# Second mixture of a two-block network: per-group picks and gates, sums added straight into the residual, 20 weight slots in place of 16, and the output's first half spread and written before the second

## The reference, cut to what matters

```python
x = x + (gates[:, :, 0] * y_rwkv + gates[:, :, 1] * y_attn) @ w_out      # the merge
h2 = rmsnorm(x, norm2_g)
...
grp = argmax(h2 @ w_router_group + b)                 # one of 4 groups
exp_logits = (h2 @ w_router_expert + b)[own group]    # 8 experts in it
top_v, top_i = lax.top_k(exp_logits, 2)
gate = grp_p * softmax(top_v)
...
yb = (silu(xblk @ w_gate[e]) * (xblk @ w_up[e])) @ w_down[e]    # 32 experts, inner width 512
y = zeros.at[row_tok].add(yb * row_w)
return x + y
```

## Time and profile before

| | |
|---|---|
| three runs | 2453.55, 2458.93, 2458.0 us; median 2458.0 |
| the profiled execution | 2457.96 us, its span 2455.9 us |
| TensorE busy | 2255.2 us (92%) |
| VectorE busy | 708.9 us (29%) |
| ScalarE busy | 319.9 us (13%) |
| mean DMA rate over the span | 297 GB/s |

### The profile page before, as it was taken

The page is one execution under the profiler, slowest core; times in us unless marked ns, Lnnn a source line. Parts: engine busy times, 40 slices in busy tenths (PEclk is TensorE's granted clock), DMA queues, the critical chain, the costliest instruction groups (busy, mean ns, idle before and its releaser), DMA issues. The chain is left out here.

```text
span 2455.9 us, 47540 instructions
## 1 busy us (share of the span) xinstructions
PE 2255.2 (92%) x21976; PEld 1376.2 (56%) x21976; DVE 708.9 (29%) x1266; ACT 319.9 (13%) x716; POOL 19.4 (1%) x17
## 2 busy tenths in 40 slices
PE   6999999999999999999999999999999997777776
PEld 5678888877544444353534344688789852222121
DVE  6763222436410101101111111455465331111110
ACT  3331000234100000000000000332222110000000
POOL 1000000100000000000000000000000000000000
PEclk9999999999999999999999999999999998877877
DMA  9568555603699999999999999333300659999997
GB/s 398 232 249 330 218 217 200 287 1 144 229 402 394 399 386 404 384 406 377 415 374 412 381 394 378 126 123 137 124 3 4 261 223 422 421 422 421 421 421 329
DMA packets 109825, 728.83 MB, mean 297 GB/s; under 512 B 12560, under 2 KB 15920, under 8 KB 34992
## 3 DMA queue, kind: packets, MB, share of 16 engines
q1 hardware_dynamic: 109040, 723.57, 73.7%
q0 software_dynamic: 576, 2.10, 0.2%
HBM read 719.30 MB, written 6.29 MB: 295 GB/s over the span
## 5 line engine op out<-in xcount | busy, mean ns | idle before, releaser
L1550 PE MATMUL bank<-ring,moe_xg 128*32 128x512 f32 (+1 forms) x6144 | 583.4, 541 | 6.1 <-DVE moe_acc L1655 5.5
L1550 PEld LDWEIGHTS bank<-ring,moe_xg 128*32 128x32 f32 x6144 | 198.8, 110 | 382.5 <-issue 372.1
L1561 PE MATMUL bank<-ring,moe_turned 128*32 128x256 f32 x5376 | 291.5, 379 | 0.0
L1561 PEld LDWEIGHTS bank<-ring,moe_turned 128*32 128x32 f32 x5376 | 174.8, 110 | 117.0 <-issue 3.1
L1946 PE MATMUL bank<-ring,moe_shared 128*32 128x512 f32 x896 | 156.9, 797 | 82.4 <-DMA ring<-stream 82.4
L1108 PE MATMUL bank<-h_chan,ring 128*128 128x256 f32 x896 | 195.6, 379 | 1.4 <-ACT h_chan L494 1.4
L1108 PEld LDWEIGHTS bank<-h_chan,ring 128*128 128x128 f32 x896 | 170.2, 190 | 24.6 <-issue 1.6
L2429 PE MATMUL bank<-h_chan,ring 128*128 128x256 f32 x672 | 148.0, 380 | 1.9 <-DVE h_chan L2534 1.9
L1666 DVE TENSOR_TENSOR moe_hidden<-moe_silu,bank 128x512 f32<-128x512 f32 (+1 forms) x48 | 26.9, 615 | 402.2 <-PE bank L1550 402.2
L2429 PEld LDWEIGHTS bank<-h_chan,ring 128*128 128x128 f32 x672 | 127.1, 190 | 23.0 <-issue 6.3
L1946 PEld LDWEIGHTS bank<-ring,moe_shared 128*32 128x32 f32 x896 | 22.2, 122 | 207.9 <-DMA ring<-stream 177.9
(11 more groups left out here) (453 smaller groups left out, 2131.3 us busy)
## 6 DMA issues: line engine op xcount, KB each, us to landing
ring<-stream SPq DMA_DIRECT2D x289, 1024.0 KB, 25.0
ring<-wide SPq DMA_DIRECT2D x240, 1024.0 KB, 8.3
ring<-wide SPq DMA_DIRECT2D x128, 768.0 KB, 6.7
ada_slots<-stream SPq DMA_DIRECT2D x28, 1024.0 KB, 7.2
late<-stream SPq DMA_DIRECT2D x24, 1024.0 KB, 27.7
rows<-zeros SPq DMA_DIRECT2D x6, 512.0 KB
moe_x_rows<-rows SPq DMA_DIRECT2D x28, 96.0 KB, 6.5
x_chan<-xT SPq DMA_DIRECT2D x1, 1024.0 KB, 15.5
```

Of the source, the lines that this page charges most:

```text
L1550: mm = self.k.nc.tensor.matmul(banks[r][i * TILE:(i + 1) * TILE, 0:width], self.m.xg[:, r, t * TILE:(t + 1) * TILE], w[:, i, :], start=(t ...
L1561: mm = self.k.nc.tensor.matmul(self.sum_bank[r][q * TILE:(q + 1) * TILE, :], self.m.turned[:, r, n * TILE:(n + 1) * TILE], w[:, f2, q * T: ...
```

## The change

1. The hybrid's `gate` and `mixed` now lie in one allocation with `late`, so that three more slots (16, 17, 18) can be laid over them and a fourth (19) over `hT`. The order becomes 20 long, and the new loads are issued in `hybrid_merge`: load 11 as before, then a wait for the 8th `h_ready`, loads 12 to 18 (the three new slots first, then slots 2, 3, 4, 0), a wait for the merge's last weights to be used, and load 19 into `hT`. The loads issued at the start of `stage_lanes` are gone.
2. Picks and gates are made for one group at a time: `dve_pick` for the next group and `dve_gated` for this one at the head of `dve_group`, two transposes on TensorE (`pe_turns`) after the up products, one copy on ScalarE (`act_turned`) after silu. `pick_rest`, `gate_slots`, `gate_turns` and `gate_out` are no longer used here.
3. `acc` is gone: `dve_collect` adds to `xT` in every group; its memset and the final addition are gone.
4. In the last group TensorE spreads quarters 0 and 1 between the fifth and the sixth down slot, quarters 2 and 3 after the last. SyncE writes each quarter to `out` as it is added. The branch now stands behind this on every engine. When it is taken, its rounds add to `xT` and write `out` again.

```diff
-RING, LATE = 14, 2
+RING, LATE, EXTRA = 14, 2, 4
...
+        room = ctx.enter_context(self.nc.sbuf_tensor("late", [P, (LATE + EXTRA) * SLOT + 6 * T], F32))
+        self.late = room[:, 0:(LATE + 1) * SLOT].rearrange("p (s n) -> p s n", s=LATE + 1)
+        self.late_gate = room[:, (LATE + 1) * SLOT:(LATE + 3) * SLOT]
+        self.late_mixed = room[:, (LATE + 3) * SLOT:(LATE + EXTRA) * SLOT + 6 * T]
...
+        extra = [self.late_gate[:, 0:SLOT], self.late_gate[:, SLOT:2 * SLOT], self.late_mixed[:, 0:SLOT],
+                 self.hT[:, :, :].rearrange("p t n -> p (t n)")]
...
-LAST_ORDER = [5, 6, 8, 9, 10, 11, 12, 13, RING, RING + 1, 7, 1, 2, 3, 4, 0]
-ISSUED = 15
+LAST_ORDER = [5, 6, 8, 9, 10, 11, 12, 13, RING, RING + 1, 7, 1, RING + 2, RING + 3, RING + 4, 2, 3, 4, 0, RING + 5]
...
-            for j in range(11, ISSUED):
+            nxt.load(sp, 11)
+            sp.wait_ge(*S("h_ready").at(DT))
+            for j in range(12, 19):
                 nxt.load(sp, j)
+            sp.wait_ge(*loads.done(loads.n - 1))
+            nxt.load(sp, 19)
...
+    def dve_pick(self, dve, g):
+        k, m, W, L = self.k, self.m, self.m.width, self.lanes
+        for t in range(TT):
+            k.nc.vector.tensor_tensor(m.pick[:, t, :].rearrange("p (e w) -> p e w", e=L),
+                                      spread(k.t("iota")[:, 1:W + 1], L), spread_last(self.own(m.place, t, g), W),
+                                      ALU.is_equal).then_inc(*self.picks_ready.up())
...
+    def pe_turns(self, pe, g):
+        pe.wait_ge(*self.mask_ready.at(g * TT + TT))
+        pe.wait_ge(*self.acc_done.at(g * 4))
+        for t in range(TT):
+            mm = self.k.nc.tensor.transpose(self.turn_bank[:, t * P:(t + 1) * P], self.m.gated[:, t, :],
+                                            self.k.t("ident"))
+        mm.then_inc(*self.turn_done.up())
+
+    def act_turned(self, act, g):
+        act.wait_ge(*self.turn_done.at(g + 1))
+        self.k.nc.scalar.activation(self.m.gate_t[:, :], self.turn_bank[:, 0:T], ACT.Copy)\
+            .then_inc(*self.turn_out.up())
...
+        self.pe_turns(pe, g)
         if not last:
             self.pe_gather(pe, g + 1, 0)
...
             mm.then_inc(loads.ring.used, 1)
-
-    def pe_spread(self, pe, g):
+            if last and j == self.per_half:
+                self.pe_spread(pe, g, range(2))
+        self.pe_spread(pe, g, range(2, 4) if last else range(4))
...
     def dve_group(self, dve, g, last=False):
         v, m = self.k.nc.vector, self.m
+        self.dve_gated(dve, g)
+        if not last:
+            dve.wait_ge(*self.mask_ready.at(g * TT + TT))
+            self.dve_pick(dve, g + 1)
...
-            for j in range(ISSUED, loads.slots):
-                loads.load(sp, j)
             loads.rest(sp)
             fullest = route.fullest(sp)
+            for q in range(4):
+                sp.wait_ge(*main.acc_done.at(4 * (G - 1) + q + 1))
+                write_out(sp, q)
             with sp.If(fullest > W):
...
-            route.dve(dve, link)
+            link(v.memset(m.place[:, :, m.experts:], 0.0))
+            route.dve(dve, link, main.dve_pick)
             main.dve_take(dve, 0, 0)
             main.dve_take(dve, 0, 1)
-            link(v.memset(m.acc[:, :, :], 0.0))
             dve.wait_ge(*route.exp_done.at(2))
             gate_weights(k, m, link)
-            pick_rest(k, m, main.lanes, link)
-            gate_slots(k, m, dve)
-            for g in range(G - 1):
-                main.dve_group(dve, g)
-                main.dve_sums_out(dve, g, main.y_ready)
-                main.dve_collect(dve, g)
-            dve.wait_ge(*main.acc_done.at(4 * (G - 1)))
-            link(v.tensor_tensor(k.xT[:, :, :], m.acc[:, :, :], k.xT[:, :, :], ALU.add))
-            main.dve_group(dve, G - 1, True)
+            for g in range(G):
+                main.dve_group(dve, g, g + 1 == G)
+                for half in range(2):
+                    main.dve_sum_out(dve, g, half)
+                    if g + 1 == G:
+                        main.dve_collect(dve, g, range(2 * half, 2 * half + 2))
+                if g + 1 < G:
+                    main.dve_collect(dve, g, range(4))
```

More of the change, by code:

```diff
@@ L2070, in _ @@
                             work.loads.load(sp, j, g)
-            for q in range(4):
-                sp.wait_ge(*S("x_out").at(q + 1))
-                sp.dma_start(out[:, 2 * q:2 * q + 2, :], k.xT[:, 2 * q:2 * q + 2, :]).then_inc(*S("out").up(16))
+                sp.wait_ge(*S("out").at(64))
+                sp.wait_ge(first.acc_done.sem, 1 + 4 * G * len(more))
+                for q in range(4):
+                    write_out(sp, q)
+                sp.wait_ge(*S("out").at(128))
             sp.wait_ge(*S("out").at(64))
@@ L2127, in _ @@
                 for work in rounds():
-                    for t in range(TT):
-                        gate_out(k, m, act, t, work.gate_banks)
                     with act.Fori(0, G) as g:
@@ L2161, in _ @@
                     v.memset(m.mark[:, 4 + i:5 + i], 0.0).then_inc(c.sem, 1)
-                main.dve_sums_out(dve, G - 1, first.y_ready)
-                more_link(v.memset(m.acc[:, :, :], 0.0))
-                for q in range(4):
-                    dve.wait_ge(first.spread_done.sem, q + 1)
-                    v.tensor_tensor(m.acc[:, 2 * q:2 * q + 2, :],
-                                    first.spread_bank[q % 2][:, :].rearrange("p (t n) -> p t n", t=2),
-                                    m.acc[:, 2 * q:2 * q + 2, :], ALU.add).then_inc(*first.acc_done.up())
+                dve.wait_ge(*S("out").at(64))
                 for work in rounds():
                     next_round(k, m, more_link)
-                    pick_slots(k, m, slice(0, work.lanes), more_link)
-                    pick_rest(k, m, work.lanes, more_link)
-                    gate_slots(k, m, dve)
+                    work.dve_pick(dve, 0)
                     work.dve_take(dve, 0, 0)
@@ L2206, in __init__ @@
         E = experts
-        self.chosen, self.gates, self.place = (sb(n, [P, TT, E]) for n in ("chosen", "gates", "place"))
+        self.chosen, self.gates = (sb(n, [P, TT, E]) for n in ("chosen", "gates"))
+        self.place = sb("place", [P, TT, E + P // width if self.block == P else E])
         self.fullest, self.fullest_int = sb("fullest", [P, 1]), sb("fullest_int", [P, 1], I32)
@@ L3232, in program @@
         plan = [("ada", ADA_FIRST, RING, 1), ("mix0", 14, RING, 1), ("dense", 42, RING, 1), ("mix1", 14, RING, 1),
-                ("hybrid", 31, HYBRID_RING, 1), ("moe2", 192, RING + LATE, 1)]
+                ("hybrid", 31, HYBRID_RING, 1), ("moe2", 192, RING + LATE + EXTRA, 1)]
+        late = k.new_ring("late_slot", [k.ring[:, p, :] for p in range(10, RING)])
+        late.skipped = ADA_FIRST
+        late_ada = Loads(late, ADA_LATE, RING - 10)
+        k.weights.slots += [None] * EXTRA
+        k.weights.arrived += late.arrived
+        k.weights.landed += late.landed
+        k.weights.owner += [None] * EXTRA
         loads = {}
@@ L3255, in after @@
             return loads[names[at]] if at < len(names) else Loads(k.weights, 0)
-        late = k.new_ring("late_slot", [k.ring[:, p, :] for p in range(10, RING)])
-        late.skipped = ADA_FIRST
-        late_ada = Loads(late, ADA_LATE, RING - 10)
         stage_setup(k, loads["ada"], after("ada"), late_ada)
```

150 lines of the change are left out of this document (60 added, 90 removed).

## The result

Before: 2457.11 us (median of 5 runs, 2453.35 to 2458.93). After: 2443.59 us (median of 5, 2440.9 to 2447.41). The ratio is 0.9949, with a 95% interval of 0.9935 to 0.9962: 9 to 16 us less. The profiled execution took 2443.33 us, its span 2441.3.

The account below looks back on a forecast made before the run. The second mixture was taken as bound by reading its 192 MiB of weights, plus a 13.56 us tail. Span 2455.90 - 9.98 + 0.15 - 4.73 = 2441.34 us, plus 2.06 outside it, gave 2443.4 us, range 2438.5 to 2450.

Parts of the forecast that it names:

- Twenty slots: Weight stream of the second mixture: four more loads land before the restart, so the last slot arrives 9.98 us earlier.
- The start of the stage: Ahead of the route's first copy: an added memset costs 0.2 us, picks return 0.05, so the first product comes 0.15 later.
- Picks and gates by the group: In each group: 1.2 us of VectorE and at most 0.60 of TensorE, all hidden, so nothing counted.
- The tail: From the last slot's arrival to the span's end: 8.83 us in place of 13.56, 4.73 less.
- the two quarters left: Last spread in the tail: 2.03 us at full clock, 3.81 at half, 2.9 taken.
- lateness of the last slot: In the tail: the early spread makes TensorE up to 2.1 us late at half clock; 0.5 taken.
- the branches of SyncE and VectorE: At the span's end: branches behind the last work stick out by 0 to 0.8 us; 0.4 taken.
- a sign of being wrong: At the end: the prediction is wrong if last write's issue to span's end is clearly over 3 us.
- first rival: In the tail: the branch gives back about 2.16 us less the 0.4 counted, with writes following it; 2445.2 us, chance 0.12.
- cold tail: In the tail: half clock throughout, 2.1 us late, branch 0.8; saves only 0.99 us; 2447.1 us, chance 0.10.
- Useless slots: In the weight stream: the new slots bring nothing and the tail alone is saved; 2453.4 us, chance 0.05.
- TensorE as the bound: In the mixture's groups: at half clock TensorE needs 62.7 us a group against the stream's 59.9; 2463 us, chance 0.03.

Follow-up runs that it names:

- e1: The changed kernel with 16 weight slots in place of 20, everything else as changed; 2453.34 us.
- e6: The changed kernel with 22 idle matmuls in place of 10 ahead of the expert counts, to keep TensorE busy before the first gather; 2442.81 us.
- e10: The changed kernel with only VectorE's branch moved early, ahead of the last group's additions; SyncE's stays behind the last write; 2440.94 us.
- e8: The changed kernel with only SyncE's branch moved early, ahead of the writes; VectorE's stays behind its last addition; 2441.82 us.
- e7: The changed kernel with both SyncE's and VectorE's branches moved early, the tail's work in both arms; 2440.86 us.
- e4: The changed kernel with all four quarters of the last group spread after the last down slot and all writes after it; 2445.37 us.
- e5: The changed kernel with 18 weight slots in place of 20, run again for a profile; 2445.8 us in one run.
- e2: The changed kernel with 18 weight slots in place of 20, none over mixed or h_chan; 2448.12 us, median of 5 runs.

## Why the prediction was right

**What bounds the kernel.** Right: an unbroken stream and a tail behind it. The span was forecast at 2441.34 us and came at 2441.30, the time at 2443.4 and came at 2443.59; that near is luck in part, since up to R the profiled execution lost 2.11 us that no one forecast, its gather won 1.42 at the clock, and three terms of the tail were off by 0.5 to 1.0 us each and nearly cancel.

**Twenty slots.** 9.98 us forecast, 10.07 measured from F to L with the rest of the change in it, 9.61 between e1 and the kernel after, for the slots alone. Linear in the slots to within 0.3 us, as worked out. The loads were through by about 1986 us in place of 1984, and the stretch to 2001 carried 8.7 MB where 7.6 was forecast; all of it lies ahead of the restart, and the execution ran 2.1 us late there.

**The start of the stage.** +0.15 forecast. The memset costs 0.17 - 0.04 = 0.13 us: 1983.77 to 1983.94 between the first memset and the copy, 1981.79 to 1981.83 before. From the first pick to the gather it takes 0.64 in place of 0.76 us, so the sum is nothing. The 2.77 us held in reserve for the gather's clock are real: 6.67, 5.25 and 3.81 us were all seen, and the last stands for the full clock in place of the 3.90 taken.

**Picks and gates by the group.** Nothing forecast; e1's 443.56 us against 444.02 shows no cost. The groups of the kernel after have the prices that were taken from neighbours (by line and shape):

```profile
L1952 PE MATMUL bank<-tab_sb,moe_gated 128*128 128x128 f32 x16 | 4.3, 356 | 0.0
L1935 DVE TENSOR_TENSOR moe_pick<-tab_sb,moe_place 128x128 f32<-128x128 f32 x16 | 4.0, 288 | 0.3
L1943 DVE TENSOR_TENSOR moe_gated<-moe_pick,moe_gates 128x128 f32<-128x128 f32 x16 | 3.9, 284 | 0.0
```

(4.0 + 3.9) / 8 = 1.0 us of VectorE a group, 1.2 forecast; 4.3 / 8 = 0.54 us of TensorE, at most 0.60.

**The tail.** 4.73 forecast, 5.10 measured. Three terms are off, two of them one way and one the other:
- the branch out of TensorE's path, 2.16 us: gone. The copy's end and the spread's start are 0.06 us apart;
- the two quarters left: 2.9 taken, 2.03 measured at full clock (2434.72 to 2436.75); the 3.81 of the other end came as 3.61 in e6;
- lateness of the last slot: 0.5 taken, none measured. The early spread did fall on the half clock (3.43 us, granted clock 0.57), two slots ran late behind it, and the last was on time;
- the branches of SyncE and VectorE: 0 to 0.8 bounded, 0.4 taken, 1.37 measured, outside its bounds. This is the term that was mis-sized. The 2.93 us that it took from TensorE are right for SyncE: in e10 they are what passes from the last issue to the end of its wait. But it let the span end there, where 0.32 to 0.41 us follow in every row of the table above; that gives 1.1 to 1.2, as e10 has it (3.61 - 2.49 = 1.12). The rest, some 0.2 us, comes with the second branch beside it. It also let the write land in 2.0 us whatever else runs, where it landed 1.1 us later beside VectorE's fetch; this decides the end in e8 only. The prediction had named this as a sign of being wrong, a stretch from the last write's issue to the end clearly over 3 us, and the stretch is 3.8 us (2437.47 to 2441.27): that part of the mechanism failed, and the sum held because the other two terms were off the other way. The Trainium skill (Runtime: NRT & Kernel Launch, section Instruction fetch mechanics) has the rule that a taken branch out of the fetched window waits for a fetch. The trace agrees in kind: a fetch starts 1.5 us behind VectorE's last addition where its branch is there (after, e8), and none where it was taken early (e7, e10);
- the early writes were said to queue behind the weight loads. They did not: the first is issued at 2430.12 us, and its packets run beside the last weights. Their cost is nothing all the same, by e4.

**The rivals.** The branch gives back 1.37 of its 2.16 us, two thirds of the first rival's price, but not by its mechanism: the writes do not follow the branch, the last one is through while SyncE is still in it. Of the cold tail the spread was seen (e6), the late last slot was not. Useless slots and TensorE as the bound are ruled out by e1 and e5, and by a stream that stays at 421 GB/s with TensorE busy 211 of 300 us.

## What to carry to other kernels

Where a stage streams weights without a gap, each slot that can be filled while the DMA engines are idle ahead of it is worth about its own transfer time (here 2.40 us measured for 2.50), and the gain can be read from the trace before: the time a load, the idle room, and the moment from which each piece of memory is free. A branch costs on the engine's path wherever it stands, here 2.9 to 3.4 us behind the last work and 5.4 us on VectorE while weights stream; move it to where the engine waits anyway for longer than that, with the remaining work in both arms. At the very end of the program it costs too, once the engine's time in it is longer than the last write's landing. A difference of 0.1% in a program this long is read from marks inside the profile and not from medians of five or six runs.

## What the hardware showed that was not expected

A code fetch can hold up one sixteenth of a write that runs beside it. In e8 fifteen of sixteen completions were there by +1.69 us; eight packets of 2 KB ran only after an 8 KB fetch, which ended at +1.83, and the sixteenth completion came at +2.80.

A branch can cost more in the middle than at the end. VectorE's took 5.43 us from its last copy to the next addition in e7, and its fetch started 3.5 us after the branch. Behind the last addition of the kernel after its branch took 3.35 us to the closing record, with the fetch 1.5 us after it. Whether the weights or the other target make the difference was not tried.

One execution of the 18-slot kernel (e2) took 5837.47 us with the same instructions; its 128x256 matmul records lasted 836 ns in place of 379 from the first to the last stage, while the granted clock read 1.0 throughout and VectorE was busy 717 us, about as elsewhere (707 us in e5). It was the first of six; the other five took 2445.88 to 2448.75 us. It is left out above, and its cause is open.
